# A decoder block and a routed mixture block on one core: attention tiles in another order, routing by rank, norm sums on GpSimd

## The reference

```python
# first block: three mixers on u = rms_norm(h) @ w_in, h = 16 meta tokens + 512 tokens
s = q @ k.T * scale            # 8 heads; a query sees all keys of its own and of earlier chunks
p = softmax(where(cid[k] <= cid[q], s, neg))
h = h + concat([y_conv, (p @ v) * silu(z), y_ret]) @ w_out

# second block, on the 512 tokens
x = x + concat([dilated_attention, silu(layer_norm(conv31(a * sigmoid(b))))]) @ w_out_2
aff = softmax(h @ w_router)                  # 512 tokens x 16 experts
gate, idx = top_k(aff.T, 64)                 # each expert takes its 64 best tokens
for e in range(16):                          # w1, w3: 1024 x 2816, w2: 2816 x 1024
    ye = (silu(h[idx[e]] @ w1[e]) * (h[idx[e]] @ w3[e])) @ w2[e]
    x = x.at[idx[e]].add(ye * gate[e])
```

## Time and profile before

| | us |
|---|---|
| median of 3 runs | 1982.38 (1982.06 to 1984.1) |
| the profiled execution, its own time | 1987.43 |
| its span in the profile | 1985.6 |
| TensorE busy | 1791.1 (90%) |
| VectorE, ScalarE, GpSimd busy | 449.9, 217.5, 15.5 |
| bytes moved | 598.53 MB, mean 301 GB/s |

### The profile page before, as it was taken

How to read it: one execution, slowest core, us unless ns; L and a number is a source line. 1 busy time by engine, 2 the same in 40 slices (tenths; PEclk the granted TensorE clock), 3 DMA queues, 4 the chain that set the end, 5 groups by cost and what they waited for, 6 DMA issues and landing times.

```text
span 1985.6 us, 20306 instructions
## 1 busy us (share of the span) xinstructions
PE 1791.1 (90%) x8230; PEld 765.0 (39%) x8230; DVE 449.9 (23%) x976; ACT 217.5 (11%) x427; POOL 15.5 (1%) x31
## 2 busy tenths in 40 slices
PE   7989999999999889999889898898988988889887
PEld 4645466543455433333323233232332323323322
DVE  2353264233553312011012010120101201101011
ACT  2031133001263200000000000000000000000000
POOL 0000001000000000000000000000000000000000
PEclk9799999999999989999999999999999999999999
DMA  6101210233114569999999999999999999999998
GB/s 225 42 30 43 85 43 1 85 109 85 66 43 168 219 265 424 424 427 425 425 425 425 425 426 426 425 425 425 426 425 426 425 425 426 426 426 425 425 425 341
DMA packets 82035, 598.53 MB, mean 301 GB/s; under 512 B 8824, under 2 KB 18168, under 8 KB 32712
## 3 DMA queue, kind: packets, MB, share of 16 engines
q1 hardware_dynamic: 81992, 597.93, 73.0%
HBM read 591.38 MB, written 2.10 MB: 299 GB/s over the span
## 4 chain that ended last, share of the span: by engine, by line
DMA 48%; PE 39%; SPq 5%; DVE 4%; ACT 2%; issue 1%; DVEq 0%; ACTq 0%
DMA arena<-in_w 48%; PE PS L1316 15%; PE PS L1827 7%; SPq L421 5%; PE PS L1719 3%; PE PS L1860 2%; PE PS L1486 1%; PE PS L1483 1%; PE PS L1644 1%; PE PS L1794 1%; PE PS L1703 1%; PE PS L1369 1%; PE PS L1691 1%; PE PS L1874 1%; ACT arena L710 1%
## 5 line engine op out<-in xcount | busy, mean ns | idle before, releaser
L1827 PE MATMUL PS<-arena 128*64 128x512 f32 (+1 forms) x3072 | 638.4, 562 | 107.5 <-DMA arena<-in_w 106.7
L1827 PEld LDWEIGHTS PS<-arena 128*64 128x64 f32 x3072 | 207.9, 136 | 538.3 <-issue 355.5
L1860 PE MATMUL PS<-arena 128*64 128x512 f32 x1408 | 324.9, 600 | 23.5 <-ACT arena L756 13.1
L1316 PE MATMUL PS<-arena 128*128 128x512 f32 (+7 forms) x880 | 329.2, 534 | 2.2 <-DVE arena L1055 0.8
L1316 PEld LDWEIGHTS PS<-arena 128*128 128x128 f32 (+1 forms) x880 | 159.2, 197 | 161.4 <-issue 150.4
L1860 PEld LDWEIGHTS PS<-arena 128*64 128x64 f32 x1408 | 115.2, 138 | 223.0 <-issue 169.4
L1281 DVE TENSOR_TENSOR arena<-arena,PS 128x1408 f32<-128x1408 f32 x16 | 25.9, 1621 | 692.7 <-PE PS L1827 692.7
L752 ACT ACTIVATE arena<-PS 128x1408 f32<-128x1408 f32 x16 | 21.5, 1343 | 742.3 <-PE PS L1827 742.3
L1290 DVE COPY arena<-PS 128x512 f32<-128x512 f32 x16 | 11.1, 692 | 328.8 <-PE PS L1860 328.8
L1874 PE MATMUL PS<-arena 64*128 64x512 f32 x256 | 76.7, 626 | 8.9 <-DVE arena L1275 8.1
L1298 DVE TENSOR_TENSOR arena<-arena,PS 128x512 f32<-128x512 f32 x128 | 77.9, 681 | 20.4 <-PE PS L1874 20.4
(11 more groups left out here) (256 smaller groups left out, 1004.7 us busy)
## 6 DMA issues: line engine op xcount, KB each, us to landing
arena<-in_w SPq DMA_DIRECT2D x384, 1408.0 KB, 34.6
arena<-in_w_in SPq DMA_DIRECT2D x5, 2048.0 KB, 8.2
arena<-in_w_in SPq DMA_DIRECT2D x8, 1024.0 KB, 6.5
arena<-in_w_out SPq DMA_DIRECT2D x4, 2048.0 KB, 7.7
arena<-arena SPq DMA_DIRECT2D x64, 67.5 KB, 2.1
arena<-in_tab SPq DMA_DIRECT2D x1, 2304.0 KB
arena<-in_w_in SPq DMA_DIRECT2D x1, 2176.0 KB, 18.6
arena<-in_x SPq DMA_DIRECT2D x4, 512.0 KB, 6.7
```

Of the source, the lines that this page charges most:

```text
L1316: i = pe.matmul(dst, lhs(k), rhs(k), start=k == 0, stop=k == KD - 1)
L1827: i = pe.matmul(PS[64 * f:64 * f + 64, bank + c // 512, 0:w], XE[:, k, :], slot[:, f * FH + c:f * FH + c + w], start=k == 0, stop=k == KD ...
L1860: ins = pe.matmul(PS[64 * d:64 * d + 64, 6, :], HT[:, j, 64 * f:64 * f + 64], W2R[:, f, j, d * 512:(d + 1) * 512], start=f == 0 and j == 0 ...
```

## The change

**Order of the tiles.** `TURNS = [2, 3, 1, 0]` sets which tile has turns 0 to 3, 4 to 7, 8 to 11 and 12 to 15, and the order of the rows after them. Banks of PSUM are given by `score_banks` and `out_bank`. The output projections of tile 2 (q = 0, 1) are issued in four halves in the turns of tile 0, which has the fewest keys. Projection q = 2 stands before the last `values`, q = 3 and 4 behind the first transposed row. The other three follow as before. `conv_in2` starts with the columns of tiles 1 to 3. GpSimd's tables for the second block now wait for `op_psum` 4 and `yo_free` 4 in place of `op_psum` 1. Three of its semaphores are merged in one (`gp_ready`).

**Norm sums.** GpSimd adds the four blocks in three additions of 128x512, for the mean and again for the squares, and TensorE makes one matmul for each. The variance moves from i = 5 to 6, and what VectorE and ScalarE do with it moves by one as well.

**Routing by rank.** The affinity of a token to expert e is written 128 times along a row (`AB`) and transposed, so that every partition has all 512 affinities. For each token VectorE counts how many are larger (or equal and earlier) in instructions that compare and add up (`accum_out`), and sums the counts to a rank. SEL is 1 where the rank is 0 to 63. Expert 0 is counted in part (`count_early`) between the output projections, the rest after the last tile (`count_last_tile`). Expert e + 1 is ranked at the start of expert e (`rank`), after four transposes that TensorE makes between w1 and w3. ScalarE scales the rows of tiles 0 to 2 to `H2N` before the last tile's square, in place of after all of them, and `gather` waits for SEL tile by tile.

```diff
+TURNS = [2, 3, 1, 0]
...
+        def score_banks(i):
+            t = TURNS[i // MH]
+            return [2 * (i % 2), 2 * (i % 2) + 1] if t == NT - 1 else [i % 2] if t == 0 else [i % 4]
...
-            gp.wait_ge(s["op_psum"], 1)
+            gp.wait_ge(s["op_psum"], 4)
+            gp.wait_ge(s["yo_free"], NT)
...
+            def add_blocks(src, ready):
+                for j in range(1, 4):
+                    gp.wait_ge(s[ready], j + 1)
+                    i = gp.tensor_tensor(LA, src[:, 0, :] if j == 1 else LA, src[:, j, :], ALU.add)
+                    if j < 3:
+                        own(i)
+                        own.settle()
+                i.then_inc(s["ln_sum"], 1)
+            add_blocks(CA, "cv_done")
+            gp.wait_ge(s["mean_psum"], 1)
+            add_blocks(LSQ, "lsq_done")
...
             for n in range(NT * 4):
-                ahead = n + 2 if n + 2 < (NT - 1) * 4 else n + 1
-                if ahead == n + 2 or (NT - 1) * 4 <= ahead < NT * 4:
-                    scores(2 * ahead), scores(2 * ahead + 1)
+                if n < 2:
+                    score_turn(n + 2)
+                if 3 <= n <= 8:
+                    score_turn(n + 1)
+                if 8 <= n <= 10:
+                    score_turn(n + 2)
+                if n == 12:
+                    pe.wait_ge(s["yo_free"], 1)
+                    pe.wait_ge(s["conv_y"], 2)
+                    pe.wait_ge(s["p_done"], 24)
+                if n >= 12:
+                    out_project((n - 12) // 2, 4 * (n % 2), 4 * (n % 2) + 4)
+                if 12 <= n < NT * 4 - 1:
+                    score_turn(n + 1)
                 if n >= 2:
                     values(n - 2)
                 turn_p(n)
             values(NT * 4 - 2)
+            out_project(2, 0, KD)
             values(NT * 4 - 1)
...
                 if i == 4:
                     pe.wait_ge(s["cv_done"], 4)
-                    for j in range(4):
-                        ins = pe.matmul(PS[:, 2, :], LN_ONES, CA[:, j, :], start=j == 0, stop=j == 3)
-                    ins.then_inc(s["mean_psum"], 1)
-                if i == 5:
-                    pe.wait_ge(s["cen_done"], 4)
-                    pe.wait_ge(s["lsq_done"], 4)
-                    for j in range(4):
-                        ins = pe.matmul(PS[:, 3, :], LN_ONES, LSQ[:, j, :], start=j == 0, stop=j == 3)
-                    ins.then_inc(s["var_psum"], 1)
+                    pe.wait_ge(s["ln_sum"], 1)
+                    pe.matmul(PS[:, 2, :], LN_ONES, LA, start=True, stop=True).then_inc(s["mean_psum"], 1)
+                if i == 6:
+                    pe.wait_ge(s["ln_sum"], 2)
+                    pe.matmul(PS[:, 3, :], LN_ONES, LA, start=True, stop=True).then_inc(s["var_psum"], 1)
...
-            for r in range(CAP // 8):
-                v8 = VAL[:, 8 * r:8 * r + 8]
-                left = PS[0:E, 6, :] if r == 0 else WK
-                own(dve.max(v8, left))
-                own.settle()
-                own(dve.match_replace(WK, v8, left, -1.0))
-                own.settle()
-            dve.tensor_scalar(MSK, WK, 0.0, None, ALU.is_lt).then_inc(s["msk_ready"], 1)
...
+            def count(t, c, bank, c0, c1, op, value, into):
+                return dve.tensor_scalar(into[:, 0:c1 - c0], PS[:, bank, c0:c1], value[:, t, :], None, op, ALU.add, accum_out=CNT[:, t, c:c + 1])
...
+            def count_last_tile(e, bank, value):
+                m = (NT - 1) * P
+                count(NT - 1, 0, bank, 0, m, ALU.is_ge, value, YE)
+                for t in range(NT - 1):
+                    count(t, 3, bank, m, S, ALU.is_gt, value, XT[:, t * P:])
+                count(NT - 1, 1, bank, m, S, ALU.is_gt, value, YE[:, m:])
+                count_equal(NT - 1, bank, value, XT[:, m:]).then_inc(s["cnt_done"], 1)
+                dve.wait_ge(s["cnt_done"], e + 1)
+                dve.tensor_reduce(RANK, CNT, AX.X, ALU.add).then_inc(s["rank_done"], 1)
+                dve.wait_ge(s["rank_done"], e + 1)
+                for t in range(NT):
+                    dve.tensor_scalar(SEL[:, t, :], iota_row[:, 0:CAP], RANK[:, t:t + 1], None, ALU.is_equal).then_inc(s["sel_ready"], 1)
...
+                if t == NT - 1:
+                    count_early(0, 6, AFF[:, :, 0:1], YE), own(count_early(1, 6, AFF[:, :, 0:1], XT))
+                    own.settle()
+                    own(count_early(2, 6, AFF[:, :, 0:1], YE))
                 residual2(2 * t + 1)
...
+                if not last_one:
+                    if first:
+                        pe.wait_ge(s["idg_ready"], 1)
+                    pe.wait_ge(s["ab_ready"], NT + 1 + e)
+                    for t in range(NT):
+                        i = turn_own(t, 7)
+                    i.then_inc(s["abT_psum"], 1)
                 up13(e, True, first)
```

302 lines of the change are left out of this document (163 added, 139 removed).

## The result

| | before | changed kernel |
|---|---|---|
| median, us | 1982.66 (1982.06 to 1984.1, 4 runs beside it) | 1958.97 (1958.24 to 1959.9, 4 runs) |
| ratio | | 0.988, 95% interval 0.9863 to 0.9897 |
| profiled execution, us | 1987.43 | 1959.5 |
| its span, us | 1985.6 | 1957.7 |
| mean granted clock | 0.985 | 0.993 |

The changed kernel is faster by 23.7 us, 1.2%. The forecast was 1959.7.

The account below looks back on a forecast made before the run. DMA bounds the expert loop, so the end follows the first expert's start. Tile order 4.5, norm sums 5.5 and routing 13.0, less 0.3 for early counts, give 22.7 us: 1982.38 becomes 1959.7 us, range 1954.5 to 1967.

Parts of the forecast that it names:

- the start of the first expert plus a constant: Expert loop: DMA is full, so bringing the first expert's start forward brings the run's end forward one for one.
- Tile order, 4.5: First attention: new tile order and moved projections fill TensorE's idle time, gaining 4.5 us, between 1 and 6.9.
- TensorE idles 54.3 - 1.7 - 45.7 = 6.9 us: First attention: its length, less the last convolution projection and TensorE's estimated work, leaves 6.9 us idle.
- Norm sums, 5.5: Norm statistics: six fewer matmuls (5.1 us) and most of a 0.98 us wait gain 5.5 us, between 2.5 and 6.1.
- a little of the chain reappears: Before the last key transposes: most of TensorE's 0.98 us wait for VectorE goes, but a little comes back.
- Routing, 13.0 less 0.3: Transposed affinities to gather: counting makes it 13.0 us shorter, bounds 10 and 14; early counts cost 0.3 us, bounds 0 and 1.5.
- The loop, 0: Expert loop: about 7 us of ranking per expert is covered by waiting for w3's chunks, so it costs 0.
- The limit of 17 us: Last projection to first expert: gains count only up to about 17 us, as four chunks finish that much before the queue moves.
- The clock: First gather: 6.43 us at the lower clock expected again; rival, clock stays up, another 3 us go, 1956.7 us, chance 0.12.
- The rival on the slower side: Expert loop: ranking becomes the bound if it takes over 31 us; 1986.7 us, chance 0.03.
- The fifteenth chunk near 692: Sign in SP's queue: the changed kernel's trace would show the fifteenth weight chunk issued near 692 us.
- with 11.8 us to spare: Expert loop: in each expert but the first two TensorE waits some 11.8 us for data, so added work is free up to that.

Follow-up runs that it names:

- e1: Kernel before with only the new tile order and the output projections moved into tile 0's turns; 1979.18 us, ratio 0.998.
- e4: Changed kernel with the new tile order but all output projections behind the attention; 1961.67 us, ratio 0.9889.
- e8: Changed kernel with useless matmuls filling TensorE's pauses except before the gather, and expert 0 gathering tokens 0 to 63 without waiting for counts; 1955.24 us, ratio 0.9857.
- e9: Changed kernel with each GpSimd addition of both norm sums made three times over; 1966.53 us, ratio 0.9919.
- e7: Changed kernel with useless matmuls in TensorE's three pauses between the last projection and the first gather; 1959.0 us, ratio 0.9875.
- e10: Changed kernel with useless matmuls in TensorE's pauses before the first gather, without the 384-column filling in the last logits; 1957.8 us, ratio 0.987.
- e5: Changed kernel with the 14 counts of each expert's ranking in the loop made six times over, same ranks; 1989.42 us, ratio 1.0029.
- e6: Changed kernel with the counts of each expert's ranking in the loop made nine times over, same ranks; 2195.35 us, ratio 1.1067.
- e2: Kernel before with only the norm sums moved to GpSimd; 1976.59 us, ratio 0.9969.
- e3: Kernel before with only the routing by rank; 1969.93 us, ratio 0.9935.

## Why the prediction held

- **What bounds the kernel, and "the start of the first expert plus a constant".** Shown, and more exactly than I had it: fifteenth chunk to end is 1270.7 to 1271.0 us in before, in the changed kernel and in e1 to e4, e8 and e9. It fails where the first expert's releases come late and the DMA rate with them (e7, e10: 1.0 to 1.2 us) and where the loop has another bound (e5, e6).
- **Tile order, 4.5.** 4.15 in the trace, 3.6 in the medians. Right in size, partly by luck. I gave the order and the projections one sum; e4 gives the larger part, 2.7 to 3.8 us, to the projections. The step that failed is "TensorE idles 54.3 - 1.7 - 45.7 = 6.9 us": it idled 3.3 us, so I had its work 3.6 us too small, scaled from one turn of tile 3; what stays idle is 1.3, not 2.4. The two errors and the 2.1 us of busy time that went as well nearly cancel.
- **Norm sums, 5.5.** 5.47 (e2). Right, again with an error inside: I read the 0.98 us of the earlier trace rows as TensorE standing still, but it is the idle time of the weight loads, and the matmuls lost 0.31 us to it. I had added 0.4 of the 0.98, as "a little of the chain reappears"; nothing reappears, the 0.31 go whole, and the two errors cancel. GpSimd's addition took 1.27 us, 1.35 with its wait, in place of my 1.1, but the cover was as forecast: done at 509.9 and wanted at 514.2, 4.3 us apart, where I had 518 and 522; both come 8 us sooner, 4.1 by the early clock and 4.15 by the tile order. By the Trainium skill's rule (SBUF — State Buffer, "SBUF: two separate sides") my estimate had been nearer 3.5; the trace shows the lock once beside these sums (1.13 us in place of 0.17), where TensorE had other work, and e9 shows four instructions stretched where the rotation is what TensorE waits for.
- **Routing, 13.0 less 0.3.** 13.2 in the trace, 12.9 in the medians. Counting took 2.6 us, against 2.7. Single counts: 0.54 us from start to start for 384 columns and 0.27 for 128, each with the 0.08 of its accumulator inside. The early counts took 2.9 us (2.8 forecast), ended at 668.66 as the last projection did, and cost no more than 0.14 us (e3).
- **The loop, 0.** Right; 5.7 us against 7. Also right was that the first expert would be longer and DMA not see it: its w3 starts 21.6 us behind its w1 in place of 19.5.
- **The limit of 17 us.** Right within what could be tried: 17 less the routing's 12.7 leaves 4.3, the windows have 4.1, and e8 used up 4.4.
- **The clock.** I had said that the gather would again take 6.43. It took 5.41, and this 1.02 us is the one term that I had at zero. The kernels without filling have 5.34 to 6.54; the changed kernel, e5 and e6, which do not differ ahead of the gather, have 5.41, 5.68 and 5.74, so at least 0.3 us belongs to the execution, and of the rest no run shows whether the shorter pause has a share. The rival was partly right: the clock can be held, but what it gives (1.9 us) is more than half given back, where the clock falls a second time.
- **The rival on the slower side** failed at its sizes. I put the point at 31 us of ranking and counted only the excess. It lies at about 27 us, as the cover is 19.1 us and a pause of this length also costs the clock 2.2, and it starts from the average of 80.0 us that an expert may take, not from 81.3.
- **The fifteenth chunk near 692.** It came at 686.79. 4.1 of the 5.2 us are the time that the profiled execution of before lost between 40 and 71 us, the rest is the gather. The median, on which I based the time, was not touched by it; the profiled execution of after lies 0.5 us over its median, not 5.

## What to carry to other kernels

Find the one instant from which the rest of the program is a constant, here the fifteenth chunk, and measure every edit as a difference to it, counted from an instant before the first edit: parts then add up to a tenth of a microsecond where medians scatter by one. Moving short turns to the end of a stage brought the larger part of its gain only when dense work was put between them. Before an idle row is booked as time lost, look whether it is of the matmuls or of the weight loads. And before work is put beside a loop "with 11.8 us to spare", add up the work that really covers it, and what the pause does to the clock.

## What the runs showed that I had not expected

- The pause of 9.85 us in e5 cost the next 16 matmuls 2.2 us more (5.78 in place of 3.60), one of 24.0 us 1.7 (5.27).
- A 128x8 instruction of VectorE was held for about 1 us by an addition on GpSimd, and e9's rotation for some 3.3 us in four instructions (L1181 to L1185), while one with a PSUM operand was not.
- The granted clock between 60 and 70 us was 0.50 in one execution and 0.71 in another, over the same work; with the rest of the stretch from 40 to 71 us that is 4.1 us in the profile, nothing in the median.
- The idle time of 0.98 us of the weight loads was 0.31 us of the matmuls.
- The loop's DMA moved 425 GB/s in the changed kernel, 415 and 408 in 710 to 730 us in e7 and e10, where the clock had fallen to 0.50 from 704 on and the releases came 1.7 us later behind the fifteenth chunk, and 425 again in e8, where the clock stayed up. No run changes the one without the other, so the cause is argued and not shown.
